# Placing fifteen convolution taps between weight pieces, squares before a piece, and halved last rows

## The reference

```python
# conv branch (channels 1024, CONV_K = 31)
u = a * sigmoid(b)
u = conv(u, dw) + dw_b                 # one filter per channel, over time
u = layer_norm(u, ln_g, ln_b)          # mean and variance over the 1024 channels
u = silu(u) * silu(gate)
return u @ w_proj
...
# peer_ffn: 8 heads x 16 picks per token out of 16384 experts
act = gelu(einsum("td,thkd->thk", x, expert_u[idx]))
y = einsum("thk,thkd->td", g * act, expert_v[idx])
```

## Time and profile before

| | us |
|---|---|
| median of three runs (lowest, highest) | 1284.18 (1283.8, 1284.25) |
| the profiled execution | 1284.4 |
| its span, first to last instruction | 1282.4 |
| TensorE busy, share of the span | 1127.3, 88% |
| VectorE busy | 969.6, 76% |
| ScalarE busy | 567.8, 44% |
| POOL busy | 559.3, 44% |
| mean granted TensorE clock | 0.977 |

### The profile page before, as it was taken

How to read it: one execution, slowest core, us unless ns; L and a number is a source line. 1 busy time by engine, 2 the same in 40 slices (tenths; PEclk the granted TensorE clock), 3 DMA queues, 4 the chain that set the end, 5 groups by cost and what they waited for, 6 DMA issues and landing times.

```text
span 1282.4 us, 15649 instructions
## 1 busy us (share of the span) xinstructions
PE 1127.3 (88%) x5606; PEld 779.8 (61%) x5606; DVE 969.6 (76%) x1962; ACT 567.8 (44%) x1038; POOL 559.3 (44%) x544
## 2 busy tenths in 40 slices
PE   6999999999989997999579887898778987777887
PEld 6989898999979997977335332353223532222322
DVE  5589989866789665677798876877768777777654
ACT  5476768654436435696423322422224222222221
POOL 0099999999300000000345544344445543434331
PEclk9999999999989998999899999899999999999999
DMA  7645444444554545625699999999999999999996
GB/s 256 213 133 165 131 145 138 146 140 157 165 196 163 179 160 166 197 99 195 242 419 424 428 427 427 395 427 426 427 427 398 427 424 427 427 428 426 421 427 265
DMA packets 127646, 374.37 MB, mean 292 GB/s; under 512 B 6864, under 2 KB 82640, under 8 KB 94672
## 3 DMA queue, kind: packets, MB, share of 16 engines
q0 software_dynamic: 36864, 268.45, 49.9%
q1 hardware_dynamic: 88496, 100.67, 24.0%
q10 hardware_dynamic: 2208, 4.24, 1.0%
HBM read 372.29 MB, written 1.05 MB: 291 GB/s over the span
## 4 chain that ended last, share of the span: by engine, by line
PE 52%; DMA 23%; DVE 15%; ACT 4%; issue 4%; SPq 0%; DVEq 0%; POOLq 0%; ACTq 0%
DMA big<-in_experts,big 18%; PE unit L728 12%; PE unit L420 11%; PE unit L422 11%; PE unit L421 11%; DVE work L1858 3%; DVE w_lo L1434 2%; DMA row<-in_experts,big 2%; DMA conv_in<-in_experts,big 2%; DVE big L1777 1%; ACT L836 1%; DVE conv_acc L1457 1%; DVE big L1774 1%; ACT probs L1177 1%; DVE big L1870 1%
## 5 line engine op out<-in xcount | busy, mean ns | idle before, releaser
L420 PE MATMUL unit<-in_hi,w_hi 128*128 128x256 f32 x1184 | 359.7, 304 | 2.7 <-DVE in_lo L1521 2.7
L421 PE MATMUL unit<-in_lo,w_hi 128*128 128x256 f32 x1184 | 336.6, 284 | 0.0
L422 PE MATMUL unit<-in_hi,w_lo 128*128 128x256 f32 x1184 | 336.6, 284 | 0.0
L1177 ACT ACTIVATE probs<-ident,big 128x128 f32<-128x128 f32 x256 | 102.8, 402 | 444.7 <-DVE big L1870 444.7
L728 PE MATMUL unit<-row,probs 128*128 128x512 f32 x512 | 249.3, 619 | 47.2 <-ACT probs L1177 47.0
L1434 DVE TENSOR_TENSOR w_lo<-w_raw,w_hi 128x2048 fp32r<-128x2048 f32 x91 | 210.5, 2319 | 70.9 <-ACT w_hi L845 70.7
L420 PEld LDWEIGHTS unit<-in_hi,w_hi 128*128 128x128 f32 x1184 | 228.9, 193 | 16.6 <-issue 14.7
L421 PEld LDWEIGHTS unit<-in_lo,w_hi 128*128 128x128 f32 x1184 | 228.9, 193 | 12.3 <-issue 12.0
L728 PE MATMUL unit<-big,probs 128*128 128x512 f32 x384 | 187.8, 622 | 48.7 <-ACT probs L1177 48.7
L422 PEld LDWEIGHTS unit<-in_hi,w_lo 128*128 128x128 f32 x1184 | 228.6, 193 | 0.0
L845 ACT CAST w_hi<-w_raw 128x2048 fp32r<-128x2048 f32 x91 | 172.7, 1903 | 105.7 <-PE unit L422 68.1
(11 more groups left out here) (256 smaller groups left out, 1341.6 us busy)
## 6 DMA issues: line engine op xcount, KB each, us to landing
w_raw<-in_w_in SPq DMA_DIRECT2D x58, 1024.0 KB, 5.2
w_raw<-in_w_mem_kv SPq DMA_DIRECT2D x8, 1024.0 KB, 5.2
w_raw<-in_w_out SPq DMA_DIRECT2D x8, 1024.0 KB, 5.1
w_raw<-in_w_query SPq DMA_DIRECT2D x6, 1024.0 KB, 5.3
w_raw<-in_w_diff_proj SPq DMA_DIRECT2D x4, 1024.0 KB, 5.3
w_raw<-in_w_x_proj SPq DMA_DIRECT2D x4, 1024.0 KB, 5.0
w_raw<-in_w_conv_proj SPq DMA_DIRECT2D x4, 1024.0 KB, 5.1
row<-in_experts,big POOLq DMA_INDIRECT x128
```

Of the source, the lines that this page charges most:

```text
L420: e.matmul(unit[:, to], *hi_hi, start=first, stop=False)
L421: e.matmul(unit[:, to], *hi_lo, start=False, stop=False)
L422: m = e.matmul(unit[:, to], *lo_hi, start=False, stop=final)
L1177: e.activation(diag_places[g % 12], ident[:, :], ACT.Copy, scale=here).then_inc(*mark("diag", g))
```

## The change

Three things. POOL does 16 taps of the shared tile instead of 12, and VectorE the other 15: four after each low part of the two pieces of `ahead(dg1)`, then four and three in `ahead(xg0)`. The conv sum follows directly, ahead of the split and the gate of xg0. Second, on both engines, the squares and the square sum stand between the first and the second piece of `ahead(dp0)` and no longer after the second. Third, the last two picks are gathered in halves from a view of the table with rows of half the length, in the order u254, u255, v254, v255; the dot product waits for the u half alone, TensorE also for the v half. VectorE computes the row numbers of the halves (2r and 2r + 1) in three small instructions at the end of the last head.

```diff
-SHARED_TILE, POOL_TAPS = 7, 12
+SHARED_TILE, POOL_TAPS = 7, 16
...
+        HALVED = (ALL_PICKS - 2, ALL_PICKS - 1)
+        half_rows = experts.rearrange("n (h d) -> (n h) d", h=2)
...  # TensorE, add_value
-                for wait in W(("diag", g), units.free(("y", t)) if first else None):
+                for wait in W(("diag", g), ("row", g) if g in HALVED else None,
+                              units.free(("y", t)) if first else None):
...  # ScalarE
-            ahead(slot["dp0"])
+            hi(slot["dp0"].pieces[0] + 2)
             for half in range(2):
...                  # the two squares
+            hi(slot["dp0"].pieces[1] + 2)
             hi(slot["dp1"].pieces[0] + 2)
...  # VectorE, choose
+                if head == len(heads) - 1:
+                    n = len(HALVED)
+                    e.scalar_tensor_tensor(out=row_f, in0=place_f[0][:, -n:],
+                                           scalar=float(PEER_KEYS), in1=place_f[1][:, -n:],
+                                           op0=ALU.mult, op1=ALU.add).then_inc(*mark("choose"))
+                    for wait in W(now("choose")):
+                        e.wait_ge(*wait)
+                    e.scalar_tensor_tensor(out=half_row[0], in0=row_f, scalar=1.0, in1=row_f,
+                                           op0=ALU.mult, op1=ALU.add)
+                    e.scalar_tensor_tensor(out=half_row[1], in0=row_f, scalar=2.0,
+                                           in1=ones[:, 0:n], op0=ALU.mult, op1=ALU.add).then_inc(
+                        *mark("choose", None, ("half rows", None)))
...  # VectorE, dot_product
-                for wait in W(("row", g), ("h3", t), work.free(("dot", g))):
+                for wait in W(("row u" if g in HALVED else "row", g), ("h3", t),
+                              work.free(("dot", g))):
...  # VectorE, the order
-            for i in range(2):
-                ahead(slot[f"dg{i}"])
-                gate_slot(f"dg{i}", half_of(q_cm, i), ("normed", f"dn{i}"))
-            convolve_some(10, shared_taps)
-            ahead(slot["xg0"])
+            ahead(slot["dg0"])
+            gate_slot("dg0", half_of(q_cm, 0), ("normed", "dn0"))
+            ahead(slot["dg1"], convolve=4, taps=shared_taps)
+            gate_slot("dg1", half_of(q_cm, 1), ("normed", "dn1"))
+            ahead(slot["xg0"], convolve=4, taps=shared_taps)
+            conv_sum()
             split_input("diff", q_cm)
             gate_slot("xg0", half_of(xq_cm, 0), ("attended", f"x{X_HEADS - 1}"))
-            convolve_some(len(shared_taps), shared_taps)
             ahead(slot["xg1"])
-            conv_sum()
...
-            ahead(slot["dp0"])
+            lo(slot["dp0"].pieces[0] + 2)
             square_sum()
+            lo(slot["dp0"].pieces[1] + 2)
             branch("dp", 0, 1)
...  # POOL
+            def gather_half(g, half):
+                i = HALVED.index(g)
+                for wait in W(("half rows", None), UV.free(g)):
+                    e.wait_ge(*wait)
+                e.indirect_dma_start(
+                    out=UV.ap(g)[:, half * D:(half + 1) * D], out_offset=None, in_=half_rows,
+                    in_offset=bass.IndirectOffsetOnAxis(ap=half_row[half][:, i:i + 1], axis=0)
+                    ).then_inc(*(mark(f"gather{g % len(rows)}", None, ("row", g), by=16) if half
+                                 else mark(f"gather u{i}", None, ("row u", g), by=16)))
...
-            for g in range(ALL_PICKS):
+            for g in range(HALVED[0]):
                 gather(g)
+            for half in range(2):
+                for g in HALVED:
+                    gather_half(g, half)
```

More of the change, by code:

```diff
@@ L263, in build @@
         cand = small[:, 256:512]
+        half_row = [small[:, 224 + 2 * i:226 + 2 * i].bitcast(U32) for i in range(2)]
+        row_f = small[:, 228:230]
         onehot = small[:, 512:1024].rearrange("p (s k c) -> p s k c", s=2, k=PEER_TOPK)
@@ L1459, in convolve_some, with ahead @@
                     i.then_inc(*mark("conv_tap", None, *done))
-            def ahead(s, between=(), convolve=3):
+            def ahead(s, between=(), convolve=3, taps=taps):
                 for part in range(PIECES):
                     lo(s.pieces[part] + 2)
-                    convolve_some(convolve)
+                    convolve_some(convolve, taps)
                     if part == 0:
```

## The result

The changed kernel takes 1274.49 us (median of six runs, 1272.9 to 1276.01), the kernel before 1283.67 beside it (1282.79 to 1284.25). The ratio is 0.9928, with a 95% interval of 0.9918 to 0.9938: 9.2 us faster. A second set, on another occasion, gave 0.9924 (0.9912 to 0.9936). I had forecast 8.0 us and 1276.2. The profiled execution took 1273.43 with a span of 1271.7, 10.7 less than the span before. That is more than the 9.2 of the medians: this execution is faster than its kernel's median, and the profiled one of the kernel before is slower than its own.

What follows compares the result with a forecast made beforehand. TensorE's idle time was taken to count in the weight phase, what follows the last bytes in the gathers. Gains of 7.3 + 0.7 = 8.0 us off 1284.4 give 1276.4, the median 0.2 lower: 1276.2, range 1273.6 to 1279.4.

Steps and rivals of the forecast that it cites:

- idle of 2.4 us ahead of the variance: TensorE reaches the variance at 379.8 but waits for the square sum until 382.2; the clock was taken to hold.
- rival A: x_res takes nothing from dp1's load, or lands beside it: variance at 380.1, gain 9.4 + 0.7, 1274.1 us; chance 17%.
- Part 1: Moved taps and early conv sum remove TensorE's stall at the conv mean: 6.2 us, plus about 2.5 from the clock.
- The wait of VectorE for POOL: VectorE's first shared tap waits for POOL's tap 15, idle from 339.5 to 342.05: 2.5 us.
- Part 2: Squares before dp0's second piece shorten the variance's chain by about 4 us; gain with the taps 7.3, ends 6.4 to 9.4.
- the landing of dp1's first piece: Weight load issued at 368.3 together with x_res at 368.7: lands between 373.5 and 376.5, taken as 375.6.
- The slack behind the variance: VectorE's low part after the variance comes at about 399.7, wanted at 400.0; up to 1 us can be lost.
- Part 3: In the gather tail, halved last rows start the last twelve matmuls at 1273.0 instead of 1273.70: 0.7 us, bounds 0 to 1.2.
- Rival B: The clock falls in the idle before the variance, giving back 2.5 to 2.8 us: 1279.0 us; chance 10%.
- Rival C: POOL's tap 15 is late by 1 to 3 us, idling dp0's start: 1277.2 to 1279.2 us; chance 10%.
- Rival D: The halves in the gather tail give nothing, as u254 lands with v254: 1276.9 us; 60% together with the forecast.
- Rival E: VectorE waits at its first shared tap until POOL is through; slower than before, 1285 us or more; chance 3%.

Runs made afterwards that it cites:

- the kernel with 12 taps: The changed kernel with 12 shared-tile taps on POOL as before and 19 on VectorE, placed 5, 5, 5, 4 behind the weight pieces: 1273.05 us, ratio 0.9911.
- the tie: The changed kernel with x_res issued on the semaphore that releases the load of dp1's first piece, ahead of xg1's tanh: 1278.86 us, ratio 0.9964.
- the repetition: The changed kernel run and profiled again with no edit: 1273.77 us (1271.76 to 1275.12).
- four halves: The changed kernel with the last four rows gathered in halves instead of two: 1272.98 us, ratio 0.9913.

## Why the prediction was right, and its wrong term

**The number.** The forecast of 8.0 us lies near the 9.2 of the medians, and that is in part luck. The sum has an idle of 2.4 us ahead of the variance that did not come; the profiles show the mechanism of rival A, with a gain at the variance of 10.25 us against 7.3 in my sum and 9.4 in the rival's. The median gain lies between the two sums and could not have told them apart.

**Part 1** held: TensorE leaves xg1 at 367.4 and starts dp0 at 367.6, right behind the mean, without waiting and at the full clock; I had 368.3. The wait of VectorE for POOL was 2.03 us instead of 2.5. POOL was through at 341.0 and not 342.05, for two reasons. The low part that blocks it began and ended 0.5 us earlier, since its load landed earlier. And POOL entered the stretch 0.6 us ahead, so that the block caught tap 14's add in this profile, where I had it catch the product ahead of it (POOL's timeline):

```profile
335.55 1.33 POOL L2204 TENSOR_SCALAR big<-conv_in,early_small 128x256 f32<-128x256 f32 x1
336.97 2.65 POOL L2208 TENSOR_TENSOR conv_acc<-conv_acc,big 128x256 f32<-128x256 f32 x1
```

I had put 0.45 us of waiting for dp0's low part on TensorE's account; it ended at 366.8, before it was wanted. That the four taps were moved to POOL was, as the kernel with 12 taps shows, worth nothing; my sum never asked what they are worth by themselves, and it should have.

**Part 2, the failed term: the landing of dp1's first piece.** I took 375.6; it was 372.0 (issued at 366.9, 5.1 us). Of the 3.6 us, 1.4 are the buffer that came free earlier and 2.2 the share that I gave to x_res and that it did not take. From the landing the chain took the 6.6 us of the sum: the square sum was ready at 378.6, 0.7 ahead of TensorE at 379.29. So the variance was not the new limit, and the 2.4 us of idle that the sum had there did not come. This is rival A, to which I gave 17%: 10.1 us. What put me wrong was the row I took for nearest. Behind mem, a weight load issued 1.9 us *later* took 6.7 us; here the load is issued 0.8 to 1.1 us *earlier* than x_res. My own issue times, 368.3 and 368.7, had the load ahead too, and I wrote "together". The runs with other orders show that this is what decides: 5.0 to 5.2 us with the head start, 9.2 in the tie, 6.0 with x_res well ahead. The Trainium skill's rule that DMAs of different engines interleave on the same 16 DMA engines ("DMA: Bandwidth & Descriptors", "Issuing engines are not separate DMA queues") fits the tie and the pair of x_res and the second load (8.4 and 9.6 us), but not the first load, which x_res left untouched though 4 us of the two lay over one another. How the engines choose is open.

The rest of part 2 held, but the edit is worth more than my "about 4 us", as it keeps the second load's delay off the variance. Without it TensorE waits 5.73 us there, 3.6 us of work run at the low clock, and of the 9.8 us that the profiles show at the first expert row 2.8 are left (635.04 against 637.81): 7.0 us.

**The slack behind the variance** was as thin as I said: in the first profile 0.2 us of waiting on a low part and 0.4 lost of 10.25, in the repetition nothing.

**Part 3** held to the tenth: 0.71 for 0.7, and the last matmuls joined to those of pick 252.

**Rival B** did not come about, but only because the idle did not. The 3.25 us in the tie and the 5.73 with the taps alone both brought 1.2 GHz. In the latter the clock fell 2.4 us after TensorE's last matmul, sooner than in any row I had. So no run shows that the clock would have held through an idle of 2.4 us, which I had called safe; the 1.51 us with the conv sum at its old place left it up. **Rival C**: POOL was earlier, not later. **Rival D** is refuted by the 0.71 us. **Rival E** has no support: once VectorE waited, POOL ran its last tap undisturbed.

## What to carry to other kernels

Two stalls in a row on one chain must be taken together: either edit alone gave 1.3 to 1.5 us, both with the halves (0.7) over 9. Interleave short work between the pieces that feed the busy engine, put a reduction that the busy engine will wait for ahead of work that it will not yet want, and look at what shares the DMA engines with the first load behind it: a head start of 1 us for the load that is needed was worth about 5 us here.

## What the runs showed of the hardware

- Two 1 MB loads from different queues, issued 0.1 us apart, land in 9.2 and 7.7 us; issued 0.7 to 1.1 us apart, the first lands in 5.0 to 5.2 and the second in 8.1 to 9.1, with a third behind them in 9.4 to 9.6 (in the changed kernel's first profile its conversion starts 10.4 us after the issue).
- The clock can fall after work has begun again: after an idle of 3.25 us it was still 1.00 for 1.5 us of matmuls and then 0.51 for 3.4. What the same idle costs varies from run to run: in the kernel before the clock fell at 372.8, work began again at 373.81, and 5.8 us of it ran at 0.50; with the halves alone, whose code is the same here, it fell at 370.1, work began at 373.39, and only 3.6 us ran at 0.50. The low clock lasted 6.8 us both times, so the earlier fall left less work under it. The 2.2 us less at half speed are 1.1 us of TensorE's time.
- Kernels that differ here by little or nothing differ at two places behind the first block: 144.1 to 146.6 us from its end to the first expert row, and 639.9 to 642.4 us from there to the last addition (where the halves take 0.7 and four halves 1.2 off). The cause of either was not looked for.
